# Dividing additions, turns and products by halves of the features in the first block of a two-block transformer kernel

## The chip, the cores and the metric

One core of a Trainium2 chip runs the whole kernel in one launch. The metric is device time in microseconds of that core; smaller is better.

## The reference, cut to what matters

Two transformer blocks of two layers each work on 256 tokens of 1024 features in float32. The change touches only the first block, whose layer is this:

```python
for l in range(DEPTH):                                  # DEPTH = 2
    h = _rms_norm(x, ln1_g[l])
    proj = jnp.einsum('bsd,dn->bsn', h, w_in[l])
    ...                                                 # three attention branches y_a, y_b, y_c
    gates = jax.nn.sigmoid(gate_logits.reshape(b, s, N_BRANCH, d))
    merged = jnp.sum(gates * jnp.einsum('bsne,ned->bsnd', y, w_branch[l]), axis=2)
    x = x + jnp.einsum('bsd,de->bse', merged, w_out[l])
    h2 = _rms_norm(x, ln2_g[l])
    ff = jnp.square(jax.nn.relu(jnp.einsum('bsd,df->bsf', h2, w_ff1[l])))
    x = x + jnp.einsum('bsf,fd->bsd', ff, w_ff2[l])
```

The second block (modulated norms, pooling, convolution, spatial gating, a dense feed-forward and then eight experts) follows and is not edited.

## The kernel before, in words

Tokens lie on partitions in two blocks of 128 (`b`), features along the free dimension in eight groups of 128 (`k`). A product needs its left operand with features on partitions, so TensorE **turns** x or `merged` first: `turn` (L1633 to L1650) makes 16 transposes of 128x128 in four pairs of feature groups, pair 0 and 2 into the PSUM bank T0, pair 1 and 3 into T1. `turned_evac` copies them to `hT`, times the norm's gain: ScalarE takes pairs 0 and 2 (L713 to L717), VectorE pairs 1 and 3 (L1027 to L1031). The norm's row factor is applied later, at the evacuation of the product, so that turning need not wait for it: ScalarE squares and sums x (L703), GpSimd takes the root (L616, L617).

TensorE's order in one layer of the first block is written out by hand, but for two loops of the engine itself (`Fori`): turn x; eight chunks of the projection, two token blocks each (L1680, 372 columns, banks G0 to G3); gates, attention and the products that go with them; the three branch products (L1877), whose result VectorE gates and adds into `merged` (L1309 to L1313); turn `merged`; the output product (L1887), with `k` outermost and the four quarters of x (`j`: half of the features times token block, banks G0 to G3) inside, so that all four quarters end together; VectorE adds the four quarters to x (`add_to_x`, L1041); turn x; the feed-forward, eight chunks of up (L1900, banks S0, S1, T0, T1) and down (L1907, into G0 to G3 across all chunks), opened and closed by four tiny matmuls (L1657, L1661); VectorE adds the four quarters with the squared norm factor (L1043); next layer. VectorE squares the relu's result for each piece of `hid` (L1334).

Weights come through SyncE's queue into a ring of four slots, each loaded when its former user has signalled on `used`. At the start SyncE loads x and then the ring (L510, L516), ScalarE's queue loads `vecs` (gains, tables and the identity matrix, L695), GpSimd's queue the routing table (L603). In layer 1, after the norm factor of the feed-forward, GpSimd's queue also loads what the second block's modulation needs (L646, L626, and twelve chunks of `ada_w`, L631), and VectorE works one or two of these chunks off behind the four squarings of each feed-forward chunk (`ada`, L1074).

## Time and profile before

| | |
|---|---|
| median of 3 runs | 2682.5 us (2679.85 to 2687.35) |
| the profiled execution's own time | 2686.67 us |
| its span | 2684.9 us, mean granted clock 0.969 |
| TensorE busy | 2510.9 us, 94% |
| VectorE, ScalarE, GpSimd busy | 669.6, 340.1, 58.7 us |
| DMA | 619.85 MB, mean 231 GB/s |

The span is the time from the first to the last instruction in the trace, and all starts below count from its beginning. A row gives start and duration in us, the engine, the line of the program, what is written from what, and how many instructions it merges; a float32 product takes two matmul instructions, a transpose one.

### The profile page before, as it was taken

To read this page: it belongs to the slowest core of one execution; us is meant where nothing else is said; L and a number is where in the kernel's file an instruction comes from. 1 tells how busy PE (TensorE), PEld (TensorE's weight loads), DVE (VectorE), ACT (ScalarE), POOL (GpSimd) and SP (SyncE) were. 2 spreads that over 40 slices of the span, in tenths; PEclk is the share of its full clock that TensorE was granted. 3 is DMA by queue.
4 is the path that set the end of the run, shared out by engine and by line. 5 is a ranking of instruction groups with operands and counts; after the bars stand their busy time and mean duration, and the time that the engine had idled before them with its cause. 6 is when DMAs were issued, how large, how long until landed. Compare 5 with 4: busy or idle time off the path is not lost.

```text
span 2684.9 us, 27524 instructions
## 1 busy us (share of the span) xinstructions
PE 2510.9 (94%) x11186; PEld 1579.1 (59%) x11187; DVE 669.6 (25%) x1491; ACT 340.1 (13%) x905; POOL 58.7 (2%) x95
## 2 busy tenths in 40 slices
PE   8999999999999999999999898798998889979997
PEld 5666466656564666666777655447994444434443
DVE  0353200011542243453334541101001101010101
ACT  1242000011530000101000111101000101000101
POOL 0000000000000000000000000000000000000000
PEclk9999999999999999998999898998998999999999
DMA  5323334334233977326664429996655999768971
GB/s 214 127 95 118 135 140 147 142 112 149 94 118 102 342 258 276 130 106 240 262 249 190 187 80 427 421 431 268 277 227 252 429 432 392 293 277 350 395 293 59
DMA packets 71317, 619.85 MB, mean 231 GB/s; under 512 B 4096, under 2 KB 4096, under 8 KB 48816
## 3 DMA queue, kind: packets, MB, share of 16 engines
q1 hardware_dynamic: 57344, 557.33, 52.2%
q0 software_dynamic: 13728, 60.14, 5.9%
q8 instruction: 80, 1.31, 0.2%
q10 hardware_dynamic: 144, 0.90, 0.1%
q14 instruction: 21, 0.17, 0.0%
HBM read 617.31 MB, written 1.05 MB: 230 GB/s over the span
## 4 chain that ended last, share of the span: by engine, by line
PE 82%; DMA 9%; DVE 4%; issue 3%; ACT 2%; POOL 1%; ACTq 0%; DVEq 0%; POOLq 0%; SPq 0%
DMA big<-in_moe_pack 8%; PE G L1907 8%; PE S L2105 7%; PE G L1680 6%; PE S L2103 5%; PE G L1696 5%; PE S L1900 4%; PE T L1900 4%; PE G L2118 4%; PE G L1877 3%; PE S L2040 3%; PE T L2040 3%; PE G L2046 3%; PE G L2116 2%; PE G L1887 2%
## 5 line engine op out<-in xcount | busy, mean ns | idle before, releaser
L2103 PE MATMUL S<-big,hT 128*64 128x256 f32 x2240 | 277.8, 392 | 67.6 <-DMA big<-in_moe_pack 42.2
L2103 PEld LDWEIGHTS S<-big,hT 128*64 128x64 f32 x2240 | 159.9, 140 | 183.5 <-issue 77.8
L1907 PE MATMUL G<-big 128*128 128x512 f32 x512 | 222.3, 592 | 0.0
L1555 DVE TENSOR_TENSOR probs<-S,probs 128x128 f32<-128x128 f32 (+2 forms) x105 | 35.5, 338 | 726.1 <-ACT probs L948 726.1
L2105 PE MATMUL S<-big,hT 128*128 128x512 f32 x448 | 201.3, 592 | 1.2 <-issue 1.2
L1696 PE MATMUL G<-big,hT 128*128 128x384 f32 x512 | 171.0, 488 | 0.0
L1680 PE MATMUL G<-big,hT 128*128 128x372 f32 x512 | 165.8, 488 | 2.5 <-DVE hT L1029 2.5
L1907 PEld LDWEIGHTS G<-big 128*128 128x128 f32 x512 | 97.3, 190 | 115.6 <-issue 114.8
L1074 DVE SCALAR_TENSOR_TENSOR big<-big,small 128x512 f32<-128x512 f32 x192 | 144.2, 751 | 6.5
L2116 PE MATMUL G<-big,pT 128*64 128x512 f32 x560 | 132.3, 593 | 8.3 <-ACT pT L953 8.3
L1680 PEld LDWEIGHTS G<-big,hT 128*128 128x128 f32 x512 | 99.7, 195 | 68.2 <-issue 8.1
L2105 PEld LDWEIGHTS S<-big,hT 128*128 128x128 f32 x448 | 82.8, 190 | 95.6 <-issue 95.6
L1696 PEld LDWEIGHTS G<-big,hT 128*128 128x128 f32 x512 | 95.8, 190 | 65.3 <-issue 4.0
L1900 PE MATMUL S<-hT,big 128*128 128x256 f32 x512 | 117.1, 388 | 0.0
L1900 PE MATMUL T<-hT,big 128*128 128x256 f32 x512 | 113.1, 379 | 0.0
L1900 PEld LDWEIGHTS S<-hT,big 128*128 128x128 f32 x512 | 99.9, 195 | 20.2 <-issue 6.7
L1334 DVE TENSOR_TENSOR big<-big 128x256 f32<-128x256 f32 x64 | 27.2, 426 | 326.0 <-ACT big L861 326.0
L1900 PEld LDWEIGHTS T<-hT,big 128*128 128x128 f32 x512 | 97.3, 190 | 13.2
L2118 PE MATMUL G<-big,pT 128*128 128x512 f32 x224 | 100.9, 593 | 3.3 <-ACT pT L953 3.3
L953 ACT ACTIVATE pT<-T 128x128 f32<-128x128 f32 (+1 forms) x98 | 30.3, 309 | 530.4 <-PE T L2089 530.4
L1877 PE MATMUL G<-big,yT 128*128 128x512 f32 x192 | 82.7, 592 | 0.0
L2040 PE MATMUL S<-hT,big 128*128 128x256 f32 x352 | 81.3, 385 | 0.0
(345 smaller groups left out, 2678.8 us busy)
## 6 DMA issues: line engine op xcount, KB each, us to landing
big<-in_moe_pack SPq DMA_DIRECT2D x112, 3072.0 KB, 15.8
big<-in_w_ff SPq DMA_DIRECT2D x32, 2048.0 KB, 7.9
big<-in_ada_w POOLq DMA_DIRECT2D x24, 2048.0 KB, 14.9
big<-in_ffn_pack SPq DMA_DIRECT2D x11, 3072.0 KB, 10.8
big<-in_gate_pack SPq DMA_DIRECT2D x16, 1536.0 KB, 6.5
big<-in_proj_pack SPq DMA_DIRECT2D x16, 1488.0 KB, 6.2
big<-in_branch_heads SPq DMA_DIRECT2D x6, 2048.0 KB, 7.8
big<-in_w_pack SPq DMA_DIRECT2D x8, 1536.0 KB, 6.2
```

Source lines behind the costliest of these rows:

```text
L1074: dve.scalar_tensor_tensor(out=out, in0=w[:, k, :], scalar=condc[:, k:k + 1], in1=out, op0=ALU.mult, op1=ALU.add).then_inc(ada_step.sem, 1)
L1680: ins = mm(G[2 * (c % 2) + b][:, 0:PROJ_N], hT[:, k, b * P:(b + 1) * P], w[:, k, :], start=(k == 0), stop=(k == KD - 1))
L1696: ins = mm(G[b if n < 4 else 1][:, 0:GATE_N], hT[:, k, b * P:(b + 1) * P], w[:, k, :], start=(k == 0), stop=(k == KD - 1))
L1877: ins = mm(G[j][:, :], yT[:, 4 * n + k, b * P:(b + 1) * P], w[:, k, half * 512:(half + 1) * 512], start=(k == 0), stop=(k == 3))
L1900: ins = mm(H4[f][:, 0:SEQ], w[:, k, f * P:(f + 1) * P], hT[:, k, :], start=(k == 0), stop=(k == KD - 1))
L1907: ins = mm(G[2 * half + b][:, :], hid[:, j, f, b * P:(b + 1) * P], w[:, f, half * 512:(half + 1) * 512], start=False, stop=False, skip_gro ...
L2040: ins = mm(H4[2 * f + piece][:, 0:SEQ], w[:, k, f * SEQ + piece * P:f * SEQ + (piece + 1) * P], hT[:, k, :], start=(k == 0), stop=(k == KD ...
L2046: ins = mm(G[2 * half + b][:, :], ffhid[:, i, f, b * P:(b + 1) * P], dn[:, f, half * 512:(half + 1) * 512], start=False, stop=False, skip_ ...
L2103: ins = mm(S[s % 2][f * FEW:(f + 1) * FEW, 0:SEQ], hTe[:, k, 0:FEW], wt[:, k, f * SEQ:(f + 1) * SEQ], start=(k == 0), stop=(k == KD - 1))
L2105: ins = mm(S[s % 2][:, :], hTe[:, k, 0:P], wt[:, k, :], start=(k == 0), stop=(k == KD - 1))
L2116: ins = mm(G[2][half * FEW:(half + 1) * FEW, :], ehid[:, s % 2, f * FEW:(f + 1) * FEW], wt[:, f, half * 512:(half + 1) * 512], start=first ...
L2118: ins = mm(G[2 + half][:, :], ehid[:, s % 2, f * P:(f + 1) * P], wt[:, f, half * 512:(half + 1) * 512], start=first, stop=last)
```

## The change

1. **Start.** The host also gives x turned (`xT`, features on partitions). SyncE loads `xT` first, then the first chunk of projection weights, then x. `vecs` comes in two parts, the columns with the gains first. ScalarE and VectorE multiply `xT` by the gain straight into `hT`; TensorE turns nothing for layer 0. The routing table is loaded after the first norm's root.
2. **Merging.** `merged_ok` is signalled per half of the features. TensorE turns the first half (pairs 0 and 1) before the last quarter of the last branch product, and the second half after two quarters of the output product.
3. **Output product.** It goes by quarters, first the lower four feature groups of all, then the upper four, and each quarter signals on its own. VectorE adds it to x at once. TensorE turns the first half of x before the last quarter, and the second half after two of the feed-forward's first four pieces, into G0 and G1.
4. **Feed-forward.** TensorE's loop is written out. The first chunk's up products go in two halves of `k`. The last chunk's last two feature groups of the down product go by quarters; in layer 0 the first half of x is turned before the last quarter, and the second half inside the first chunk of layer 1's projection. The tiny opening and closing matmuls go.
5. **Projection.** TensorE's loop is written out too, and its first chunk divided in halves of `k`. ScalarE squares x between its copies of the turned pairs.

```diff
-            sp.dma_start(x[:], t["x"][0].rearrange("(b p) d -> p b d", p=P)).then_inc(x_in.sem, 16)
+            sp.dma_start(xT, t["xT"].rearrange("p (k s) -> p k s", k=KD)).then_inc(xT_in.sem, 16)
...
                 for c in range(8):
                     load(l, c, slot(c)[:, 0:KD * PROJ_N], t["proj_pack"][l, c])
+                    if l == 0 and c == 0:
+                        sp.dma_start(x[:], t["x"][0].rearrange("(b p) d -> p b d", p=P)).then_inc(x_in.sem, 16)
...
-            pool.dma_start(route[:], t["route"]).then_inc(route_in.sem, 16)
...
                 norm_root(l * 2)
+                if l == 0:
+                    pool.dma_start(route[:], t["route"]).then_inc(route_in.sem, 16)
...
-            act.dma_start(vecs[:], t["vecs"]).then_inc(consts_in.sem, 16)
-            act.wait_ge(x_in.sem, 16)
+            act.dma_start(vecs[:, 0:V_BC], t["vecs"][:, 0:V_BC]).then_inc(cols_in.sem, 16)
+            act.dma_start(vecs[:, V_BC:], t["vecs"][:, V_BC:]).then_inc(consts_in.sem, 16)
...
+                if l:
+                    turned_pair(l * 2, 0, xn_turned, T[0], hT_act, gainc[l][0])
+                    square_rows(l * 2, 0)
+                    turned_pair(l * 2, 2, xn_turned, T[0], hT_act, gainc[l][0])
+                    square_rows(l * 2, 1)
...
+            dve.wait_ge(cols_in.sem, 16)
+            dve.wait_ge(xT_in.sem, 16)
+            for i in (1, 3):
+                for k in (2 * i, 2 * i + 1):
+                    ins = dve.tensor_scalar(hT[:, k, :], xT[:, k, :], gainc[0][0][:, k:k + 1], None, ALU.mult)
+                ins.then_inc(hT_dve.sem, 1)
+            dve.wait_ge(consts_in.sem, 16)
+            dve.wait_ge(x_in.sem, 16)
...
-                                if (n, j) == (2, 3):
+                                if n == 2 and b == NB - 1:
                                     ins.then_inc(merged_ok.sem, 1)
                                 else:
                                     step.did(ins)
+                            if (n, j) == (2, 2):
+                                turned_pair(l, 1, mg_turned, T[1], mg_dve, None)
                     if n:
                         step.settle()
-                turned_evac(l, mg_turned, mg_dve, None)
-                dve.wait_ge(used[23 % NSLOT].sem, used_at(l, 23))
-                add_to_x(l * 2 + 1)
-
-                turned_evac(l * 2 + 1, xn_turned, hT_dve, gainc[l][1])
+                turned_pair(l, 3, mg_turned, T[1], mg_dve, None)
+                dve.wait_ge(x_new.sem, added(l * 2))
+                for j in range(4):
+                    if j < 3:
+                        dve.wait_ge(br_mm.sem, br_mm.at(l, 9 + j + 1))
+                    else:
+                        dve.wait_ge(used[23 % NSLOT].sem, used_at(l, 23))
+                    add_quarter(j)
+                    if j == 1:
+                        turned_pair(l * 2 + 1, 1, xn_turned, T[1], hT_dve, gainc[l][1])
+                turned_pair(l * 2 + 1, 3, xn_turned, G[1], hT_dve, gainc[l][1])
...
-                dve.wait_ge(ff2_mm.sem, ff2_mm.at(l, 1))
-                add_to_x(l * 2 + 2, small[:, 306:308])
+                dve.wait_ge(x_new.sem, added(l * 2 + 1))
+                for i, j in enumerate(QUARTERS[l]):
+                    if i < 3:
+                        dve.wait_ge(ff2_mm.sem, ff2_mm.at(l, i + 1))
+                    else:
+                        dve.wait_ge(used[39 % NSLOT].sem, used_at(l, 39))
+                    add_quarter(j, small[:, 306:308])
+                    if (l, i) == (0, 1):
+                        turned_pair(l * 2 + 2, 1, xn_turned, T[1], hT_dve, gainc[l + 1][0])
+                if l == 0:
+                    turned_pair(l * 2 + 2, 3, xn_turned, T[1], hT_dve, gainc[l + 1][0])
...
+            def turn_pair(i, src, bank, turned):
+
+                for kk in range(2):
+                    for b in range(NB):
+                        k = 2 * i + kk
+                        ins = pe.transpose(bank[:, kk * SEQ + b * P:kk * SEQ + (b + 1) * P], src[:, b, k * P:(k + 1) * P], ident[:])
+                ins.then_inc(turned.sem, 1)
...
-                turn(l * 2, x, x_new, added(l * 2), xn_turned, hT_act, hT_dve, whole=False)
...
+                pe.wait_ge(hT_act.sem, hT_act.at(l * 2, 1))
+                pe.wait_ge(hT_dve.sem, hT_dve.at(l * 2, 1))
+                weights(l, 0)
+                pe.wait_ge(proj_act.sem, l * 8 + 1)
+                proj_part(0, 0, 0, KH)
+                if l:
+                    pe.wait_ge(x_new.sem, added(l * 2))
+                    turn_pair(2, x, T[0], xn_turned)
+                    turn_pair(3, x, T[1], xn_turned)
+                pe.wait_ge(proj_dve.sem, l * 8 + 1)
+                proj_part(0, 1, 0, KH)
+                pe.wait_ge(hT_act.sem, hT_act.at(l * 2, 2))
+                pe.wait_ge(hT_dve.sem, hT_dve.at(l * 2, 2))
+                proj_part(0, 0, KH, KD).then_inc(proj_mm.sem, 1)
+                proj_part(0, 1, KH, KD).then_inc(used[0].sem, 1)
+                for c in range(1, 8):
+                    weights(l, c)
+                    pe.wait_ge(proj_act.sem, l * 8 + c + 1)
+                    proj_part(c, 0, 0, KD).then_inc(proj_mm.sem, 1)
+                    pe.wait_ge(proj_dve.sem, l * 8 + c + 1)
+                    proj_part(c, 1, 0, KD).then_inc(used[c % NSLOT].sem, 1)
...
-                turn(l, merged, merged_ok, merged_ok.at(l, 1), mg_turned, mg_act, mg_dve)
...
-                turn(l * 2 + 1, x, x_new, added(l * 2 + 1), xn_turned, hT_act, hT_dve)
-                open_banks()
-                with pe.Fori(0, 4) as it:
...
+                            if (n, j) == (2, 2):
+                                pe.wait_ge(merged_ok.sem, merged_ok.at(l, 1))
+                                turn_pair(0, merged, T[0], mg_turned)
+                                turn_pair(1, merged, T[1], mg_turned)
...
+                pe.wait_ge(mg_act.sem, mg_act.at(l, 1))
+                pe.wait_ge(mg_dve.sem, mg_dve.at(l, 1))
+                weights(l, 21)
+                weights(l, 22)
+                for j in range(4):
+                    pe.wait_ge(br_ev.sem, br_ev.at(l, 8 + j + 1))
+                    if j < 3:
+                        out_part(j, 0, KH)
+                    else:
+                        out_part(j, 0, 3).then_inc(used[21 % NSLOT].sem, 1)
+                        out_part(j, 3, KH)
+                    if j == 1:
+                        pe.wait_ge(merged_ok.sem, merged_ok.at(l, 2))
+                        turn_pair(2, merged, T[0], mg_turned)
+                        turn_pair(3, merged, T[1], mg_turned)
+                pe.wait_ge(mg_act.sem, mg_act.at(l, 2))
+                pe.wait_ge(mg_dve.sem, mg_dve.at(l, 2))
+                weights(l, 23)
+                v = l * 2 + 1
+                for j in range(3):
+                    out_part(j, KH, KD).then_inc(br_mm.sem, 1)
+                pe.wait_ge(x_new.sem, 4 * v + 2)
+                turn_pair(0, x, T[0], xn_turned)
+                turn_pair(1, x, T[1], xn_turned)
+                out_part(3, KH, 6).then_inc(used[22 % NSLOT].sem, 1)
+                out_part(3, 6, KD).then_inc(used[23 % NSLOT].sem, 1)
...
+                for c in range(8):
+                    weights(l, 24 + 2 * c)
+                    if c == 0:
+                        pe.wait_ge(hT_act.sem, hT_act.at(v, 1))
+                        pe.wait_ge(hT_dve.sem, hT_dve.at(v, 1))
...
+                            pe.wait_ge(ff_relu.sem, ff_relu.at(l, f + 1))
+                            up_part(c, f, 0, KH)
+                            if f == 1:
+                                pe.wait_ge(x_new.sem, added(v))
+                                turn_pair(2, x, G[0], xn_turned)
+                                turn_pair(3, x, G[1], xn_turned)
+                        pe.wait_ge(hT_act.sem, hT_act.at(v, 2))
+                        pe.wait_ge(hT_dve.sem, hT_dve.at(v, 2))
+                    for f in range(4):
+                        pe.wait_ge(ff_relu.sem, ff_relu.at(l, 4 * c + f + 1))
+                        up_part(c, f, KH if c == 0 else 0, KD).then_inc((ff_mm if f < 3 else used[2 * c % NSLOT]).sem, 1)
+                    weights(l, 25 + 2 * c)
+                    for f in range(4 if c < 7 else 2):
+                        pe.wait_ge(ff_ev.sem, ff_ev.at(l, 4 * c + f + 1))
+                        for j in range(4):
+                            ins = down_part(c, f, j)
+                    if c < 7:
+                        ins.then_inc(used[(2 * c + 1) % NSLOT].sem, 1)
+                pe.wait_ge(ff_ev.sem, ff_ev.at(l, 32))
+                for i, j in enumerate(QUARTERS[l]):
+                    if (l, i) == (0, 3):
+                        pe.wait_ge(x_new.sem, 4 * (v + 1) + 2)
+                        turn_pair(0, x, T[0], xn_turned)
+                        turn_pair(1, x, T[1], xn_turned)
+                    for f in (2, 3):
+                        ins = down_part(7, f, j)
+                    ins.then_inc((ff2_mm if i < 3 else used[39 % NSLOT]).sem, 1)
```

The order of the instructions shows it at three places; T0, T1, S0, S1 and G0 to G3 are PSUM banks, "waits" names the signals. First TensorE from the last quarter of the last branch product to the output product, before:

```order
L1877 MATMUL G3<-big,yT 128x512 [waits br_ev]
L1877 MATMUL G3<-big,yT 128x512 x3
L1647 MATMUL T0<-vecs,big 128x128 [waits merged_ok]
L1647 MATMUL T0<-vecs,big 128x128 x3
L1647 MATMUL T1<-vecs,big 128x128 x4
L1647 MATMUL T0<-vecs,big 128x128 [waits mg_act]
L1647 MATMUL T0<-vecs,big 128x128 x3
L1647 MATMUL T1<-vecs,big 128x128 [waits mg_dve]
L1647 MATMUL T1<-vecs,big 128x128 x3
L1887 MATMUL G0<-big,hT 128x512 [waits loaded1,mg_dve,mg_act]
L1887 MATMUL G1<-big,hT 128x512
L1887 MATMUL G2<-big,hT 128x512
```

and now:

```order
L1953 MATMUL G2<-big,yT 128x512 [waits br_ev]
L1953 MATMUL G2<-big,yT 128x512 x3
L1721 MATMUL T0<-vecs,big 128x128 [waits merged_ok]
L1721 MATMUL T0<-vecs,big 128x128 x3
L1721 MATMUL T1<-vecs,big 128x128 x4
L1953 MATMUL G3<-big,yT 128x512 [waits br_ev]
L1953 MATMUL G3<-big,yT 128x512 x3
L1965 MATMUL G0<-big,hT 128x512 [waits loaded2,loaded1,br_ev,mg_dve,mg_act]
L1965 MATMUL G0<-big,hT 128x512 x3
L1965 MATMUL G1<-big,hT 128x512 [waits br_ev]
L1965 MATMUL G1<-big,hT 128x512 x3
L1721 MATMUL T0<-vecs,big 128x128 [waits merged_ok]
```

The eight transposes of `merged`'s first half now stand before the last quarter of the branch product, those of the second after two half-quarters of the output product, which is itself reordered. Then TensorE from the output product to the feed-forward, before:

```order
L1887 MATMUL G2<-big,hT 128x512
L1887 MATMUL G3<-big,hT 128x512
L1647 MATMUL T0<-vecs,x 128x128 [waits x_new]
L1647 MATMUL T0<-vecs,x 128x128 x3
L1647 MATMUL T1<-vecs,x 128x128 x4
L1647 MATMUL T0<-vecs,x 128x128 [waits hT_act]
L1647 MATMUL T0<-vecs,x 128x128 x3
L1647 MATMUL T1<-vecs,x 128x128 [waits hT_dve]
L1647 MATMUL T1<-vecs,x 128x128 x3
L1657 MATMUL G0<-zcol,vecs 128x2 [waits hT_dve,hT_act]
L1657 MATMUL G1<-zcol,vecs 128x2
L1657 MATMUL G2<-zcol,vecs 128x2
```

and now:

```order
L1965 MATMUL G2<-big,hT 128x512 x4
L1721 MATMUL T0<-vecs,x 128x128 [waits x_new]
L1721 MATMUL T0<-vecs,x 128x128 x3
L1721 MATMUL T1<-vecs,x 128x128 x4
L1965 MATMUL G3<-big,hT 128x512 x4
L1999 MATMUL S0<-hT,big 128x256 [waits hT_dve,ff_relu,hT_act,loaded0]
L1999 MATMUL S0<-hT,big 128x256 x3
L1999 MATMUL S1<-hT,big 128x256 [waits ff_relu]
L1999 MATMUL S1<-hT,big 128x256 x3
L1721 MATMUL G0<-vecs,x 128x128 [waits x_new]
L1721 MATMUL G0<-vecs,x 128x128 x3
L1721 MATMUL G1<-vecs,x 128x128 x4
```

The turns of x stand apart, each between matmuls that do not wait for it, and the zcol matmuls are gone. Third, VectorE from the additions to x to the feed-forward; `used3` is the last quarter's signal. Before:

```order
L1041 TENSOR_TENSOR x<-G0,x 128x512 [waits x_new,used3]
L1041 TENSOR_TENSOR x<-G2,x 128x512
L1041 TENSOR_TENSOR x<-G1,x 128x512
L1041 TENSOR_TENSOR x<-G3,x 128x512
L1029 TENSOR_SCALAR hT<-T1,vecs 128x256 [waits xn_turned]
L1029 TENSOR_SCALAR hT<-T1,vecs 128x256
L1029 TENSOR_SCALAR hT<-T1,vecs 128x256 [waits xn_turned]
L1029 TENSOR_SCALAR hT<-T1,vecs 128x256
```

and now:

```order
L1068 TENSOR_TENSOR x<-G0,x 128x512 [waits br_mm,x_new]
L1068 TENSOR_TENSOR x<-G1,x 128x512 [waits br_mm]
L1053 TENSOR_SCALAR hT<-T1,vecs 128x256 [waits xn_turned]
L1053 TENSOR_SCALAR hT<-T1,vecs 128x256
L1068 TENSOR_TENSOR x<-G2,x 128x512 [waits br_mm]
L1068 TENSOR_TENSOR x<-G3,x 128x512 [waits used3]
L1053 TENSOR_SCALAR hT<-G1,vecs 128x256 [waits xn_turned]
L1053 TENSOR_SCALAR hT<-G1,vecs 128x256
```

The additions to x stand one by one with their own waits, and the copies of the turned pairs between them.

## Rows read from the trace of the kernel before

**Rows 1.** Chain of waits, whole run: start us, us, engine and line, how many instructions.
```profile
16.26 82.76 PE G L1680 x256
...
256.63 41.22 PE G L1877 x96
303.36 30.02 PE G L1887 x64
341.04 8.70 PE S L1900 x32
349.74 6.91 PE T L1900 x32
356.64 13.73 PE G L1907 x32
...
571.93 83.10 PE G L1680 x256
...
814.34 41.22 PE G L1877 x96
860.61 27.72 PE G L1887 x64
897.68 9.18 PE S L1900 x32
```

**Rows 2.** Chain of waits, from the end of layer 0's feed-forward.
```profile
563.20 0.80 PE G L1661 x8
...
564.03 2.74 DVE x L1043 x4
```

**Rows 3.** Timeline, ScalarE, a projection evacuation: start us, us, engine, line, idle before.
```profile
44.13 0.57 ACT L732 ACTIVATE big<-G,small 128x372 f32 x1 [9.41 <-PE G L1680]
```

**Rows 4.** Chain of waits, first 30 us.
```profile
0.76 7.75 DMA x<-in_x
...
8.68 1.28 ACT L722
...
10.18 2.08 ACT yT L703 x4
```

**Rows 5.** DMA issues of the first 30 us, then one stretch (last columns: PEclk, DMA share, GB/s).
```profile
big<-in_proj_pack SPq DMA_DIRECT2D x5, 1488.0 KB, 13.6
...
vecs<-in_vecs ACTq DMA_DIRECT2D x1, 879.0 KB, 5.8
route<-in_route POOLq DMA_DIRECT2D x1, 232.0 KB, 6.9
...
12.00:16.00 4.00, 1.97 (x8) 1.57 (x8) 0.95 (x3) 1.82 (x6) 0.91 (x2) 1.00 1.01 432
```

**Rows 6.** Timeline, TensorE in attention: transposes, then scores; then that stage's stretch.
```profile
132.08 1.04 PE L1785 MATMUL T<-vecs,probs 128*128 128x128 f32 x8
133.05 1.14 PE L1765 MATMUL S<-big 64*128 64x256 f32 x8
...
124.00:148.00 24.00, 23.00 (x122) 14.11 (x124) 12.29 (x32) 13.86 (x47) 0.00 (x0) 1.00 0.26 97
```

**Rows 7.** Timeline, GpSimd's and VectorE's part in the modulation's chunks; landing of two chunks.
```profile
894.39 1.79 POOL L631 DMA_DIRECT2D big<-in_ada_w  x2
...
DMA to landing us min/median/max: 18.1/20.4/22.6
...
914.56 12.63 DVE L1074 SCALAR_TENSOR_TENSOR big<-big,small 128x512 f32<-128x512 f32 x16
931.40 0.43 DVE L1334 TENSOR_TENSOR big<-big 128x256 f32<-128x256 f32 x1 [4.21 <-ACT big L861]
```

**Rows 8.** Waits of TensorE: us in total, times, longest us.
```profile
PE S L2103 <- issue: 23.5, 4, 10.8
```

**Rows 9.** Stretches after the output product's start, layers 0 and 1.
```profile
303.36:333.38 30.02, 30.01 (x64) 12.97 (x64) 0.00 (x0) 0.00 (x0) 0.00 (x0) 0.92 0.43 158
860.61:888.33 27.72, 27.70 (x64) 12.05 (x64) 0.00 (x0) 0.00 (x0) 0.00 (x0) 1.00 0.55 198
```

More of the change, by code:

```diff
@@ L80 @@
 FT = 2
+KH = KD // 2
+QUARTERS = ((0, 1, 2, 3), (0, 2, 1, 3))
 ROW_L1 = 2 * KD + KCQ + KCKV
@@ L426, in added @@
         def added(n, b=NB - 1):
-            return 4 * n + 2 * b + 2
+            return 4 * n + (3 + b if n < U_MIX else 2 * b + 2)
         def used_at(l, pos):
@@ L1032, in turned_evac @@
-                    ins.then_inc(done.sem, 1)
-            def add_to_x(n, mul=None):
-                dve.wait_ge(x_new.sem, added(n - 1))
-                for b in range(NB):
-                    for half in range(2):
-                        xs = x[:, b, half * 512:(half + 1) * 512]
-                        if mul is None:
-                            dve.tensor_tensor(xs, G[2 * half + b][:, :], xs, ALU.add).then_inc(x_new.sem, 1)
-                        else:
-                            dve.scalar_tensor_tensor(out=xs, in0=G[2 * half + b][:, :], scalar=mul[:, b:b + 1], in1=xs, op0=ALU.mult, op1=ALU.add).then_inc(x_new.sem, 1)
+                    turned_pair(v, i, turned, T[1], done, mul, add)
@@ new lines, in up_part, with down_part @@
+                def up_part(c, f, k0, k1):
+                    w = slot(24 + 2 * c).rearrange("p (k n) -> p k n", k=KD)
+                    for k in range(k0, k1):
+                        ins = mm(H4[f][:, 0:SEQ], w[:, k, f * P:(f + 1) * P], hT[:, k, :], start=(k == 0), stop=(k == KD - 1))
+                    return ins
+                def down_part(c, f, j):
+                    half, b = divmod(j, 2)
+                    w = slot(25 + 2 * c).rearrange("p (k n) -> p k n", k=4)
+                    return mm(G[j][:, :], hid[:, c % 2, f, b * P:(b + 1) * P], w[:, f, half * 512:(half + 1) * 512],
+                              start=(c == 0 and f == 0), stop=(c == 7 and f == 3))
```

137 lines of the change are left out of this document (68 added, 69 removed).

## Prediction

> **What bounds the kernel now.** The table of busy time comes first: TensorE works 94% of the span, so only its idle stretches and its slow stretches can be won. The chain of waits over the whole run is read next [rows 1]. In the first block it is TensorE almost throughout, in long unbroken pieces; what the change can touch are the seams between them. There are five where x or `merged` is turned, and each is the distance from the end of one piece to the start of the next. Merging, layer 0: 256.63 + 41.22 = 297.85 to 303.36, 5.51 us. Merging, layer 1: 855.56 to 860.61, 5.05. Output product to feed-forward, layer 0: 333.38 to 341.04, 7.66. The same in layer 1: 888.33 to 897.68, 9.35. Feed-forward to layer 1's projection: 563.20 [rows 2] to 571.93, 8.73. Together 36.3 us. In the last of them VectorE's four additions, which all start when the last quarter is ready, take 2.74 us alone [rows 2]; the rest is turning, copying and turning again.
>
> Each seam has a second price, seen behind it [rows 1, 9]. After the merging of layer 0 the 64 matmul instructions of the output product take 30.02 us at a granted clock of 0.92; the same in layer 1 takes 27.72 at 1.00. A piece of 32 such instructions takes 13.73 in steady state, so 64 take 27.46: the lower level of the clock (1.2 instead of 2.4 GHz), granted after TensorE stood idle, cost 2.56 and 0.26 us. The first up piece behind the next seam takes 8.70 and 9.18 instead of 6.91: 1.79 and 2.27. The projection of layer 1 takes 83.10; one evacuation of 0.57 and an idle wait of 9.41 make 9.98 us per chunk [rows 3], 79.9 for eight, so 3.2 is lost. Together 10.1 us.
>
> **The start.** x lands at 8.51 and the first product begins at 16.26 [rows 1, 4]; between them lie ScalarE's table load (1.28 us), two squarings that hold up its copies (2.08), and turning in two rounds. With `xT` nothing of this stands before the product but the table load and the multiplications, four to an engine, of which the first two are enough. What stands there instead is the first chunk of weights, until now covered. By 8.51 the queues had moved x (1024 KB), `vecs` (879) and the routing table (232) [rows 4, 5]. Without the table, 232 KB at 432 GB/s earlier, and with the chunk's 1488 KB behind, its weights are there at 8.51 - 0.55 + 3.53 = 11.5; I take 11.6 for the product, a gain of **4.7 us**. Bounds: if the second part of `vecs` takes no share ahead of it, near 9.9 (gain 6.4); if x, queued behind, takes its full share, 2.4 later (gain 2.3). The queues moved what lay ahead and no more by 8.51, so I take the middle. x then lands near 14, is squared by 16.5, and its root is needed only when the first quarter of the projection is complete, some 9 us after its start: hidden. The second chunk of weights, near 17.5, is needed near 24. The products at the low level, which the first ones also were, stay.
>
> **The five seams.** The transposes themselves stay on TensorE. In attention eight of them, between matmuls, take 0.97 us from first start to the next instruction's [rows 6], so 16 take 1.94 and five seams 9.7. All else in the seams I cost at nothing, and name the cover. Merging: the first half is turned after the third quarter of the last branch product; the copies (under 1 us on either engine) lie under the fourth quarter, an eighth of 27.46, 3.4 us. The second half's additions lie under two half-quarters, 6.9 us, its copies under two more. Output to feed-forward: an addition (a quarter of the 2.74 us) lies under the next half-quarter; the first half's copies under the last one; the second half's addition under two up pieces, 3.5 us. There VectorE waits for the turned pair with the third quarter's addition queued behind, which nobody needs before the second turn. Feed-forward to projection: the cover is one down quarter, 1.7 us, for copies of 0.9, the tightest place; then four projection matmuls, 2.5 us. If any cover is short, tenths are lost. So the seams give 36.3 - 9.7 = **26.6 us**, less about 0.1 for each of ten blocks of transposes: **25.6**. Bounds: 26.6, and 21 if each block stands open by 0.5.
>
> **The clock.** With no idle stretch of more than tenths, I take all **10.1 us** back; between nothing and this.
>
> **The end of layer 1's feed-forward.** The closing matmuls (0.80 us, as in layer 0 [rows 2]) go, and three of four additions are done before the last quarter, 2.1 us of 2.74. The next product also waits for the modulation's own matmuls and copies, which move only by the 0.80. I take **1.5**, between 0.8 and 2.9.
>
> **Moved work that might cost.** Slots 2 and 3 of the ring come free together at the end of the output product, instead of apart; their loads are needed 29 us later (one up and one down chunk), so nothing. GpSimd's routing load waits for the first root; nobody asks for it in this block. Layer 1's chunks for the modulation are issued after the norm's root, which now comes after the second turn inside the feed-forward instead of before it. Before, they were issued at 894.39, 3.3 us ahead of the first up product; now at least two up pieces and a turn behind it, 4.4, and by a square (half of 2.08 [rows 4]) and a root more, so some 7: 10 us later. Two chunks landed after 18.1 to 22.6 us and VectorE worked on them from 914.56 for 12.63 us, then stood idle 4.2 us before the next squaring [rows 7]. The squaring's result is needed only by the next down product, another 10 us on. Cost nothing; the rival below has the price.
>
> Sum: 4.7 + 25.6 + 10.1 + 1.5 = 41.9, so **42 us**. The profiled execution's own time, 2686.67, becomes 2644.7; it lay 4.2 above the median of the runs, 2682.5, from which I get 2640.5 and forecast **2641**. The second block only shifts: each of its loads waits for TensorE's own progress.
>
> **Rivals.**
> 1. *The clock falls all the same.* Ten blocks of transposes of a microsecond each might count as standing idle. For it: the low level followed seams in which TensorE turned much of the time. Against it: in attention, with such blocks among the products, the granted clock is 1.00 [rows 6]. It takes the 10.1 us away: 2651. The Trainium skill's page "TensorE: Matmul & The Clock Gate", section "Part 4: PE-mode transpose", says that a transpose does not count as busy in the way a product does; by that rule the time is this rival's. The stretch of attention does not bear it out for short blocks.
> 2. *VectorE is late with the modulation's chunks.* If a chunk is 15 us later, VectorE ends its two chunks after the next down product wants its squares. For it: 4.2 us of slack before the squaring. Against: another 10 us behind it. Price 1 to 8 us: 2646.
> 3. *Gains swallowed later*: a load in the second block that runs by itself would give the time back there. Nothing in the chain shows one; 2682, no change.
> 4. *Slower: written-out code must be fetched.* TensorE's loops ran 16 chunks a layer from two or four bodies; now each chunk has its own code. Where TensorE entered other code in the expert stage it waited for nothing that the profile shows, 23.5 us in 4 times [rows 8], 5.9 each. One such wait in each of 16 feed-forward chunks is 94 us, so 2735; it decides from the eighth wait on. Against it: attention is written out, and TensorE was busy 23.0 of 24 us there [rows 6]. The Trainium skill's page "Runtime: NRT & Kernel Launch", section "Instruction fetch mechanics", says that fetching runs ahead in sequence and that taken branches break it; by this rule the rival falls away. No run here shows fetching by itself.
>
> **Chances.** Forecast 0.72, clock 0.12, VectorE 0.09, swallowed 0.04, fetch 0.03. A measurement tells 0.3% (8 us) from no change; the first three are all faster, 0.93, then 0.04 the same and 0.03 slower. The range takes in the forecast with its bounds (start 1.7 more, end 1.4, blocks 1, and 3 to 5 us between runs: 2630), the clock rival, and that rival with VectorE's price: **2630 to 2660**.
>
> **What would show it.** First product near 11.6; the ends and starts of the pieces 2 us apart at each seam, all of it transposes; the output product, with its turns taken off, at 27.5 us in both layers; first up pieces at 6.9; granted clock 1.00 behind the seams. Layer 1's second feed-forward chunk tells rival 2 by a wait of TensorE for VectorE; a gap without a releaser in the written-out loops tells rival 4. I would be wrong if the seams closed and the span shrank by less than 30 us, or if they stayed open by more than 3 us each.

## The result and the profile after

| | before | changed |
|---|---|---|
| time, median of 4 runs each | 2684.76 us (2679.85 to 2687.35) | 2649.25 us (2644.59 to 2653.8) |
| ratio | | 0.987, 95% interval 0.9846 to 0.9894 |
| profiled execution, its span | 2686.67, 2684.9 | 2649.68, 2647.9 |
| mean granted clock of the span | 0.969 | 0.975 |

The kernel is faster by 35.5 us in the medians and by 37.0 in the two profiled spans. The forecast was 42 off the span, and 2641 with a range of 2630 to 2660 for the time.

First the chain of waits of the changed kernel over the whole run, its long pieces in the first block (start us, us, engine and line, instructions), beside [rows 1]:

```profile
1.20 10.71 DMA big<-in_proj_pack
...
12.16 83.15 PE G L1733 x256
...
254.58 37.77 PE G L1953 x88
...
551.38 77.52 PE G L1733 x248
...
866.83 30.67 DMA big<-in_ada_w
...
904.27 16.27 PE G L2006 x32
...
934.35 13.73 PE G L2006 x32
...
1098.21 7.14 PE G L2077 x32
```

The first product now starts at 12.16, 4.1 earlier, and what it waits for is the first chunk of weights (the row of 10.71). Two rows are new in kind: a DMA of `in_ada_w` stands in the chain at 866.83 for 30.67 us, and the down product behind it takes 16.27 where its neighbours take 13.73. That is the place where the change lost time.

How a seam looks now, first between output product and feed-forward in layer 0, then between feed-forward and projection, from the same view in two short windows:

```profile
321.57 0.88 PE T L1721 x8
322.44 3.44 PE G L1965 x8
325.88 3.45 PE S L1999 x16
329.33 0.87 PE G L1721 x8
330.21 3.46 PE T L1999 x16
...
546.29 1.72 PE G L2006 x4
548.01 2.50 PE G L1733 x8
550.51 0.87 PE T L1721 x8
```

Every row starts where the last one ended. The eight transposes (L1721) take 0.87 or 0.88 us, and nothing else is left of the seam. The windows say the same (PE, PEld, DVE, ACT and POOL busy, then PEclk, DMA share and GB/s); the first three lie over seams, the fourth behind the last of them:

```profile
296.00:342.00 46.00, 46.00 (x158) 27.75 (x157) 8.59 (x18) 6.05 (x14) 0.89 (x2) 1.00 0.51 183
528.00:560.00 32.00, 32.00 (x111) 19.19 (x110) 6.80 (x15) 5.20 (x11) 0.89 (x2) 1.00 0.27 98
828.00:870.00 42.00, 42.00 (x144) 24.93 (x143) 7.57 (x15) 5.29 (x12) 3.98 (x6) 1.00 0.63 228
870.00:905.00 35.00, 30.75 (x109) 20.58 (x108) 14.10 (x22) 2.30 (x6) 1.76 (x2) 0.96 1.03 400
```

TensorE is busy in 46.00 of 46.00, 32.00 of 32.00 and 42.00 of 42.00 us. In the fourth it is busy for 30.75 of 35, while the DMA engines are full (share 1.03, 400 GB/s).

Where the 37.0 us came from, as distances between the starts of pieces in the two chains:

| term | forecast | measured |
|---|---|---|
| first product (16.26 to 12.16) | 4.7 | 4.1 |
| five seams and the clock behind them | 35.7 | 37.5 |
| end of layer 1's feed-forward (15.23 to 12.38) | 1.5 | 2.85 |
| modulation chunks late | 0 | -6.8 |
| all else (layer 0's projection, attention, second block) | 0 | -0.7 |
| sum | 42 | 37.0 |

The second row is made of these: branch product to first up product 84.41 to 71.30 in layer 0 and 83.34 to 71.30 in layer 1; layer 0's feed-forward to the next projection 230.89 to 222.13; layer 1's projection 83.10 to 80.89, its turn included; together 36.1. To these come 1.4 that layer 1's feed-forward would have given without its wait: it took 222.64 before and 228.05 now, and eight periods of 27.55 (the distance between the starts of down products in steady state) with a turn of 0.87 are 221.27. 228.05 - 221.27 is the loss of 6.8.

The loss itself, first in the waits of TensorE between 780 and 1130 us (line waited at, engine and line waited for: us in total, times, longest):

```profile
PE G L2006 <- DVE big L1376: 4.3, 1, 4.3
```

and then in VectorE's timeline, which answers to [rows 7] (start us, us, line, operation, idle before and its releaser):

```profile
889.08 6.26 DVE L1101 SCALAR_TENSOR_TENSOR big<-big,small 128x512 f32<-128x512 f32 x8 [15.73 <-DMA big<-in_ada_w]
897.52 6.27 DVE L1101 SCALAR_TENSOR_TENSOR big<-big,small 128x512 f32<-128x512 f32 x8 [2.18 <-DMA big<-in_ada_w]
903.70 1.43 DVE L1376 TENSOR_TENSOR big<-big 128x256 f32<-128x256 f32 x4
```

VectorE stands 15.73 us waiting for a chunk. Its program puts chunks 0 and 1 ahead of the squarings of the second feed-forward block, so these squarings run as four at once at 903.70, and the down product that wanted the first of them at 900.02 waits 4.3 us. Then it takes 16.27 instead of 13.73: 2.5 us more at the low level. 4.3 + 2.5 is the 6.8.

Why the chunks came so late shows in GpSimd's timeline:

```profile
863.93 0.69 POOL L623 TENSOR_TENSOR small<-small,mhalf 128x2 f32<-128x2 f32 x1
...
865.38 0.56 POOL L632 DMA_DIRECT2D big<-in_ada_bias  x1
865.93 1.79 POOL L637 DMA_DIRECT2D big<-in_ada_w  x2
```

and in the landing of these two chunks:

```profile
DMA to landing us min/median/max: 23.1/26.9/30.7
```

The issue moved from 3.3 us ahead of the first up product to 8.2 behind it (857.78), 11.4 later; the landing of the second chunk grew from 22.6 to 30.7, 8.1 more. In the kernel before, VectorE was still at work on the first chunk for 3 us after the second had landed, and that hid 3 of it. 11.4 + 8.1 - 3.0 = 16.5, and the end of the two chunks indeed lies 46.0 us behind the first up product where it was 29.5. Why the landing grew is told by the queues between issue and landing of the second chunk (queue: packets, MB, share of the 16 engines' time), q0 being GpSimd's, q1 SyncE's. Before, 895.27 to 917.9 us:

```profile
q0 software_dynamic: 1471, 8.38, 93.8%
q1 hardware_dynamic: 279, 0.60, 7.1%
```

and in the changed kernel, 866.83 to 897.5 us:

```profile
q0 software_dynamic: 1472, 8.39, 68.4%
q1 hardware_dynamic: 1496, 3.90, 33.7%
```

GpSimd's queue moves the same in both, the band, the bias and two chunks. SyncE's moves 3.30 MB more, and the engines together 398 GB/s before and 402 now: 3.30 MB are 8.2 us at that rate, the whole growth. 2.10 MB of the 3.90 are the load of weights issued at 872.69, when the first feed-forward chunk's up products are done; it landed after 23.1 us, within the stretch. Most of the rest is left of the two loads issued together at 856.25 and 857.98.

The end of the last feed-forward, in the chain:

```profile
1085.85 0.76 DVE x L1070
```

One addition stands there; before it were the closing matmuls and four additions in a row.

### The profile page after: what moved, and what is told of

Same layout as the page of the kernel before. It is cut to its first block, busy times and chain, and to the rows that moved or that the text cites. A ratio compares the mean times of both kernels' runs of the same rounds, so it can differ in the third digit from the quotient of the medians.

```text
span 2647.9 us, 27348 instructions
## 1 busy us (share of the span) xinstructions
PE 2484.4 (94%) x11138; PEld 1560.8 (59%) x11139; DVE 669.9 (25%) x1491; ACT 340.6 (13%) x906; POOL 58.5 (2%) x95
## 4 chain that ended last, share of the span: by engine, by line
PE 82%; DMA 10%; DVE 3%; issue 2%; ACT 1%; POOL 1%; ACTq 0%; SPq 0%; DVEq 0%; POOLq 0%
DMA big<-in_moe_pack 9%; PE G L2006 8%; PE S L2236 7%; PE G L1733 6%; PE S L2234 5%; PE G L1771 5%; PE S L1999 4%; PE T L1999 4%; PE G L2249 4%; PE G L1953 3%; PE S L2171 3%; PE T L2171 3%; PE G L2177 3%; PE G L2247 2%; PE S L2300 2%
## 5 line engine op out<-in xcount | busy, mean ns | idle before, releaser
L1606 DVE TENSOR_TENSOR probs<-S,probs 128x128 f32<-128x128 f32 (+2 forms) x105 | 35.5, 338 | 729.7 <-ACT probs L975 729.7
L1999 PE MATMUL S<-hT,big 128*128 128x256 f32 x512 | 113.4, 379 | 0.0
L2171 PE MATMUL S<-hT,big 128*128 128x256 f32 x352 | 79.6, 379 | 0.0
```

What stands on the lines that cost most here:

```text
L1999: ins = mm(H4[f][:, 0:SEQ], w[:, k, f * P:(f + 1) * P], hT[:, k, :], start=(k == 0), stop=(k == KD - 1))
L2171: ins = mm(H4[2 * f + piece][:, 0:SEQ], w[:, k, f * SEQ + piece * P:f * SEQ + (piece + 1) * P], hT[:, k, :], start=(k == 0), stop=(k == KD ...
```

## The experiments

**1. Modulation chunks early.** The changed kernel, with the bias and the first two chunks issued in layer 1 as soon as merging is complete, the band later:

```diff
+                if l == DEPTH - 1:
+                    pool.wait_ge(merged_ok.sem, merged_ok.at(l, 2))
+                    load_modulation(0, 0, 2)
...
-            load_modulation(0)
+            load_modulation(0, 2)
```

> The changed kernel, but GpSimd issues the bias and the first two chunks of the modulation's weights as soon as merged is complete in layer 1, before the norm's root; the band table comes behind them. Theory (late chunks): in the changed kernel VectorE waited 15.7 and 2.2 us for chunks, TensorE then 4.3 us for VectorE, and the next down product took 16.27 instead of 13.73 us at the low clock. Without this 6.8 us go: about 2642 against 2649, no wait of TensorE on the squaring, down products at 13.73. Rival (DMA contention): the weights of the output product and the feed-forward, loaded at the same time, come late instead and TensorE waits for them: 2649 or more.

Measured: 2644.76 us (2639.61 to 2645.66), ratio to before 0.9848 (0.9834 to 0.9862). Span 2643.7, that is 4.2 under the changed kernel's. The 6.8 us are all there in layer 1's feed-forward: it takes 221.26 us instead of 228.05, and TensorE waits for no squaring. The edge in question, in VectorE's timeline:

```profile
871.06 12.62 DVE L1105 SCALAR_TENSOR_TENSOR big<-big,small 128x512 f32<-128x512 f32 x16
```

Both chunks are worked on without idle time before them, where the changed kernel had 15.73 and 2.18 us, and are done at 883.68.

Up to the end of that feed-forward this run is ahead of the changed kernel by 9.0 us (1076.84 against 1085.83), of which 2.0 come from the first projection and attention, whose low level differs from one execution to the next (below). Behind it, the next product took 8.77 us instead of 7.14, at the low level, and the second block some 3 us more. So the loss is located and removed, while the total moved by less than the place did.

**2. Chunks late in the kernel before.** The same mechanism from the other side: the band, bias and chunks are held back.

```diff
+            pool.wait_ge(ff_relu.sem, ff_relu.at(DEPTH - 1, 4 + 1))
             pool.dma_start(rot[:, 2048:4096], t["band"]
```

> The kernel before, with GpSimd's loads of the modulation held back until the first relu of layer 1's feed-forward, some 10 us later; nothing else changed. Theory (late chunks): the same loss as in the changed kernel appears without any of its reordering, TensorE waits 3 to 6 us for the squaring and then runs slow: plus 5 to 8 us, 2689 to 2693. Rival (the written-out loop or the quarters caused the wait): no difference from before, 2684.

Measured: 2682.21 us, ratio 0.9998 (0.9988 to 1.0007). No effect; the expectation missed. VectorE's timeline:

```profile
921.91 6.26 DVE L1075 SCALAR_TENSOR_TENSOR big<-big,small 128x512 f32<-128x512 f32 x8 [11.84 <-DMA big<-in_ada_w]
930.05 6.26 DVE L1075 SCALAR_TENSOR_TENSOR big<-big,small 128x512 f32<-128x512 f32 x8 [1.88 <-DMA big<-in_ada_w]
936.24 1.42 DVE L1335 TENSOR_TENSOR big<-big 128x256 f32<-128x256 f32 x4
```

VectorE waits for the chunks as it should, but the squarings begin at 936.24 and the down product that wants them starts at 936.80, less than 0.1 us behind the up product (its end is at 936.74). The slack was used up exactly. The issue lay 8.2 us behind the first up product (900.92 against 892.69), as in the changed kernel, and the second chunk landed after 28.2 us instead of 22.6: SyncE's queue moved 2.92 MB beside it, though its loads are spaced here as before. A later issue thus brings most of the longer landing with it, and the two together use up the slack and no more. The changed kernel's wait needs the rest: its second chunk landed after 30.7 us, and it wants the squares 42.2 us behind its first up product instead of 44.0, because that block no longer runs at the low level. 2.5 and 1.8 are the 4.2 between the two waits, to a tenth.

**3. Two groups later still.** To see whether the wait begins past that edge:

```diff
-            pool.wait_ge(ff_relu.sem, ff_relu.at(DEPTH - 1, 4 + 1))
+            pool.wait_ge(ff_relu.sem, ff_relu.at(DEPTH - 1, 4 + 3))
```

> This is the kernel before with the band, the bias and the modulation chunks of layer 1's feed-forward held back until the third rectified group of the first block, two groups (6.9 us) later than in the run with them held to the first. There the two squarings of VectorE ended in the very microsecond in which TensorE wanted them. Theory (VectorE's order puts two chunks ahead of the squarings, so a chunk that lands later than that run's is paid by TensorE one for one): TensorE waits 6 to 7 us for VectorE's squaring before the down product of the second block, and that product runs at the low level or partly at it for 0 to 2.5 us more; 2689 to 2692 us. Rival (the wait in the changed kernel came from the two queues' collision in the DMA engines, not from order and lateness): no wait of TensorE above 1 us, 2682 to 2685.

Measured: 2695.8 us (2685.65 to 2700.69), ratio 1.0043 (1.0029 to 1.0056). The waits of TensorE, then the chain:

```profile
PE G L1908 <- DVE big L1335: 8.0, 1, 8.0
```

```profile
907.88 29.22 DMA big<-in_ada_w
...
943.88 16.05 PE G L1908 x32
```

Against experiment 2 the chunks are issued 6.8 us later, counted from the first up product, and land after 29.2 us instead of 28.2. That gives 7.8 of the 7.9 more of waiting (8.0 against under 0.1), and again a down product at the low level, 16.05. The chain has the same DMA row as the changed kernel's. The span is 9.8 above the last run's, about what these two make (7.9 and 2.1). The median is 4 us above what was expected; the runs lie over 15 us, and that part is not explained. The rival (collision alone) falls: in the kernel before, whose loads of weights are spaced as ever, order and lateness are enough. No run takes away only the bunching of the two loads that SyncE now issues together. Without it the landing is 28.2 and 29.2 us here and in experiment 2, so it can account for the last 1.5 to 2.5 of the 30.7.

**4. Loops written out.** The kernel before, with TensorE's two hardware loops unrolled and nothing else:

```diff
-                with pe.Fori(0, 2) as it:
+                for it in range(2):
...
-                with pe.Fori(0, 4) as it:
+                for it in range(4):
```

> The kernel before, with TensorE's two loops (projection and feed-forward) written out and nothing moved. Theory: code that runs straight on costs nothing here: 2684, within 3 us. Rival (fetch): gaps of 5.9 us with no releaser in the written-out stretches, slower by tens of us.

Measured: 2686.3 us, ratio 1.0008 (0.9998 to 1.0017). Its waits of TensorE include

```profile
PE S L2103 <- issue: 24.0, 5, 10.7
```

as in [rows 8] (23.5 us): no new gap without a releaser in the feed-forward. Up to 1130 us, where the written-out loops stand, its matmuls have no wait of 0.3 us or more without a releaser. Writing out costs nothing that can be measured, at most 4.6 us by the interval.

**5. The start alone.** The kernel before with `xT`, `vecs` in two parts, and the routing table later:

```diff
-            sp.dma_start(x[:], t["x"][0].rearrange("(b p) d -> p b d", p=P)).then_inc(x_in.sem, 16)
+            sp.dma_start(xT, t["xT"].rearrange("p (k s) -> p k s", k=KD)).then_inc(xT_in.sem, 16)
...
+            act.wait_ge(cols_in.sem, 16)
+            act.wait_ge(xT_in.sem, 16)
+            for i in (0, 2):
+                for k in (2 * i, 2 * i + 1):
+                    ins = act.activation(hT[:, k, :], xT[:, k, :], ACT.Copy, scale=gainc[0][0][:, k:k + 1])
```

> The kernel before with the start of the changed kernel alone: x loaded turned, gains first, routing table later. Theory: the first product starts at 12.2 instead of 16.3, all else follows 4 us earlier: 2680.5 or so. Rival (the start was hidden by something later, or the later x holds up the first evacuation): no difference, 2684.

Measured: 2677.64 us against 2682.89, ratio 0.998 (0.9971 to 0.9989). The chain starts

```profile
1.20 10.62 DMA big<-in_proj_pack
...
11.94 1.60 PE G L1701 x2
```

so 4.3 us earlier than 16.26, and the median agrees (5.2 lower).

**6. Seams filled.** The kernel before keeps its seams, but TensorE multiplies an unused tile in them, into a bank that nobody reads:

```diff
+            def fill(n):
+                for _ in range(n):
+                    mm(S[1][:, 0:384], ident[:], vecs[:, 0:384], start=True, stop=True)
```

> The kernel before, with idle time in the five seams filled by matmuls whose result nobody reads (identity times the gain columns, into bank S1): two ahead of the first turn of merged and four ahead of that of x, one or two in the later waits of a turn. The output is unchanged. Theory (the low clock behind a seam comes from idle time): the clock stays up, the pieces behind the seams take 27.5, 6.9 and 80 us; of the 10.1 us some 8 to 10 come back, less 1 or 2 for fillers that overrun: 2675 to 2679. Rival (the clock falls for another reason, such as the transposes): the pieces stay slow, and the time is 2684 or up to 4 us more.

Measured: 2675.98 us, ratio 0.9969 (0.9958 to 0.9981), 7.2 us in medians, without closing a single seam. The pieces behind the seams:

```profile
304.78 27.72 PE G L1895 x64
...
340.14 7.01 PE S L1908 x32
...
568.52 80.23 PE G L1688 x256
...
889.65 7.01 PE S L1908 x32
```

against 30.02, 8.70, 83.10 and 9.18 in [rows 1]. With the idle time filled and the transposes left in place the pieces run at full speed, so here it was idle time that lowered the clock. But the other runs on the kernel before, whose seams stand open (experiments 2 to 5), show that two of these four rows were a draw: a low level that one profiled execution has and another of the same code has not. The output product of layer 0 took 29.71 in experiment 2 and 27.72 in the other three, and layer 1's projection took 80.25 to 80.28 in all four. Only the first up piece is slow every time (8.70 to 9.41 us behind layer 0's seam, 9.18 to 9.60 behind layer 1's). So what is lost reliably is 1.8 to 2.7 us behind the output seam in each layer. Of the forecast's 10.1, 5.2 (30.02 - 27.72 and 83.10 - 80.25) are lost in some executions and not in others. The low level also lengthens the seams from within: in layer 1's output seam of the kernel before, eight transposes took 1.98 us and eight closing matmuls 1.84, and with fillers 1.11 and 1.02. The five seams, 36.3 us long before, are 33.3 here, so some 3.0 of what the forecast counts as seams was clock. The low level behind a seam that is filled or closed was seen in none.

**7. x turned whole.** The changed kernel with the seam between output product and feed-forward put back:

```diff
-                turn_pair(0, x, T[0], xn_turned)
-                turn_pair(1, x, T[1], xn_turned)
...
+                turn(v, x, x_new, added(v), xn_turned, hT_act, hT_dve)
...
-                                turn_pair(2, x, G[0], xn_turned)
-                                turn_pair(3, x, G[1], xn_turned)
```

> The changed kernel, but x is turned whole between output product and feed-forward, after all four additions, with the quarters of the output product kept. Theory: the seam opens again by the last addition (0.7), two rounds of copies (about 1 and 1.1) and the clock falls in some of the two: plus 3 to 5 us a layer, 2655 to 2659. Rival (only ending the product by quarters mattered, the halves of the turn did nothing): within 2 us of the changed kernel's 2649.

Measured: 2650.79 us, ratio 0.9883 (0.9868 to 0.9898), 1.5 above the changed kernel instead of 6 to 10. By the total this is the rival's number, but the chain tells otherwise. It shows the seam (the output product ends at 322.30):

```profile
301.68 20.62 PE G L1964 x48
...
326.81 3.69 PE S L1996 x16
```

From branch product to the next layer's projection it is 296.43 us instead of 293.43: 3.0 lost in layer 0. In layer 1 the same distance to the end of the feed-forward is 295.79 instead of 299.35: 3.6 gained. TensorE has no wait for a squaring there, and the second down product takes 13.95. The seam gives the modulation's chunks the time that they lack, and so hides its own price.

**8. x turned whole and chunks early.** Experiments 7 and 1 together, to see the seam without that cover:

> This is the changed kernel with both single edits together: x turned whole between output product and feed-forward, and the first two modulation chunks fetched early in layer 1. Theory (the seam itself costs 3.0 us in each layer, 6.0 in all, and the run with x turned whole alone came out only 1.5 us above the changed kernel because the same edit removed the 6.8 us that TensorE had waited and run slowly for the chunks): with the wait gone on both sides, branch product to the end of the last down product in layer 1 takes 292.5 + 3.0 = 295.5 us here, the same 3.0 us longer branch product to layer 1's projection in layer 0 (296.4), and the run is about 6 us above the 2644.8 of the early chunks alone, 2649 to 2652. Rival (the divided turn of x gains nothing, the seam is worth under 1 us): 2644 to 2647, with stretches of 293.4 and 292.5 us.

Measured: 2650.07 us, ratio 0.9869 (0.9853 to 0.9885), 5.3 above the 2644.76 of the early chunks alone. In the chain, from branch product (254.19) to projection (548.90 + 1.72 = 550.62) 296.43 us; from branch product in layer 1 (789.09) to the end of the feed-forward (1084.66) 295.57, against 292.56 in experiment 1: 3.0 us for each of these seams, as expected. The rows of experiment 7 give the same price: the seam from 322.30 to 326.81 is 4.51 us, turning included, then TensorE takes 3.69 instead of 3.45 for 16 matmuls, and saves two blocks of transposes, 1.75, of the divided version. 4.51 + 0.24 - 1.75 = 3.0. This prices the divided turn of x alone. What ending the output product by quarters gave, and the seams of merging and of the next projection, is read from the chain and was not taken back by itself.

**9. Transposes fourfold.** The changed kernel with each block of eight transposes issued four times:

```diff
-                for kk in range(2):
+                for kk in range(2 * 4):
+                    kk = kk % 2
```

> The changed kernel with each block of eight transposes repeated four times in place (it writes the same values again; output unchanged). Nine such blocks of 0.87 us become 3.5 us each. Theory (transposes keep the clock up like other matmuls): plus 9 times 2.6, 23 us, 2672, granted clock 1.00 behind the blocks. Rival (transposes count as idle): matmuls behind the blocks run at the low level, 2 to 3 us more for each, 2690 to 2699.

Measured: 2665.18 us, ratio 0.9939 (0.9924 to 0.9955); span 2663.4, 15.5 more than the changed kernel's, at a mean granted clock of 0.978. One seam, from the chain:

```profile
303.19 3.49 PE T L1722 x32
306.69 17.17 PE G L1966 x40
323.86 3.50 PE T L1722 x32
...
330.79 3.45 PE S L2000 x16
```

A block takes 3.5 us, 2.62 more, and every product behind one runs at full speed: 17.17 for 40, 3.45 for 16. The window over this stretch has clock 1.00:

```profile
296.00:342.00 46.00, 46.00 (x198) 29.49 (x197) 6.89 (x14) 4.52 (x10) 0.89 (x2) 1.00 0.51 182
```

From branch product to projection layer 0 takes 306.54 instead of 293.43, five blocks of 2.62. Ten blocks, where the expectation counted nine, make 26.2. The total grew by only 15.5, not by the 23 expected, because layer 1's chunks are again less late (TensorE waits 1.3 us instead of 4.3, and the down product takes 13.97), 5.2 us in all, and because start, first projection, attention and second block happen to be 5.5 shorter. The rival, that transposes let the clock fall, is not borne out.

**10. The best version.** Experiment 1, with the second part of `vecs` issued by ScalarE after its copies of `xT`, so that it takes no share ahead of the first weights:

```diff
-            act.dma_start(vecs[:, V_BC:], t["vecs"][:, V_BC:]).then_inc(consts_in.sem, 16)
...
                 ins.then_inc(hT_act.sem, 1)
+            act.dma_start(vecs[:, V_BC:], t["vecs"][:, V_BC:]).then_inc(consts_in.sem, 16)
```

> The early chunks of the other run, and the second part of vecs (687 KB) issued by ScalarE after its copies instead of at once. Theory: the first weights land some 1.6 us earlier (687 KB at 432 GB/s), first product near 10.5, the gains at 9 to 10 just cover it: 2640 to 2641. Rival: hT, ready near 9.8, or the tables, needed by VectorE, hold up something: no better than 2642.

Measured: 2639.29 us (2637.68 to 2643.66), ratio 0.984 (0.9827 to 0.9853), span 2637.5, 10.4 under the changed kernel's.

```profile
1.20 8.93 DMA big<-in_proj_pack
...
10.37 2.82 PE G L1737 x4
```

1.8 us come from the start (10.37 against 12.16), 6.8 from layer 1's feed-forward; the rest is 2.7 from the first projection and attention, where the low level is a draw, less 0.9 elsewhere. All five runs of it lie below every run of the changed kernel.

## Why the prediction held, and where it was off

**The start** was read rightly, by its middle: 4.1 of 4.7. That the second part of `vecs` takes part of the share ahead of the weights, kept in the forecast as the bound of 6.4, is what the last experiment turns into 1.8 us.

**The seams** closed as forecast. No cover ran short, the tightest one of 1.7 us for copies of 0.9 included. The transposes were the over-costed part: taken at 0.97 from attention, and at 0.1 more for each block, they cost 0.87. Two per seam in five seams, 1.07 - 0.87 each, make 2.0 us, and that is why seams and clock gave 37.5 instead of 35.7. (The lower bound for open blocks, 26.6 less ten times 0.5, is 21.6 and not 21.)

**The clock** came back in full, as the step said; the filled seams show that idle time was its cause. Some 3.0 us of the 26.6 booked as seams were clock as well (experiment 6). But of the 10.1 us I read from one profiled execution, about half was not there in the other executions of the same seams. The two spans, from which 37.0 comes, contain it, and the medians (35.5) only in part. A low level that is a draw shows in attention as well. There scores of eight instructions behind a wait take 1.94 and 1.99 us at the low level, 1.14 and 1.13 else: in layer 1 before, in layer 0 after. With the eight behind them (1.71 and 1.69 instead of 0.86) it costs 1.7 us in either kernel and cancels. That row, of the changed kernel's chain in layer 0:

```profile
120.23 1.94 PE S L1840 x8
```

The one place of [rows 6], a little later in the same layer before, ran at the full level.

Rival 1 falls: blocks of up to 3.5 us of transposes between products did not bring the granted clock down (1.00 in experiment 9). The Trainium skill's page "TensorE: Matmul & The Clock Gate", section "Part 4: PE-mode transpose", says that a transpose does not count as busy in the way a product does; this kernel does not bear that out for blocks of this length, and longer ones were not tried.

**The end** gave 2.85 where I took 1.5, the upper of the two bounds. The one addition left takes 0.76 us ([rows 2] had 2.74 for four).

**The chunks** are the step that failed: "Cost nothing; the rival below has the price". Rival 2, at 0.09, came true, and its price of 1 to 8 us holds the 6.8. The slack was read rightly, 4.2 before the squaring and some 10 behind it. What was mis-sized is how late the chunks would be: 10 us were forecast and 16.5 came, against 14. The issue was 11.4 later, near enough. But the landing was taken to be as it was, and it grew by 8.1, because SyncE's queue moved 3.90 MB beside it instead of 0.60. Of this some 5.6 us come with the later issue itself (experiment 2) and up to 2.5 with the two loads that now go out together. The sentence about these, "needed 29 us later, so nothing", priced them for their own consumer only, and not for who shares the DMA engines with them. A price was also missing from the wait: the low level in the down product behind it, 2.5 us, which the argument on the seams should have supplied. Experiments 1 to 3 show the mechanism from both sides: taken away, 6.8 gained in place; made in the kernel before, nothing up to the edge and then one for one.

**Swallowed later** (rival 3) falls, since the second block took 1549.69 us after 1549.35. **Fetch** (rival 4) falls by experiment 4. The Trainium skill's page "Runtime: NRT & Kernel Launch", section "Instruction fetch mechanics", says that fetching runs ahead in sequence, and experiment 4 agrees: no wait of 0.3 us or more without a releaser in the written-out loops, and a ratio of 1.0008.

**The total** is in part luck: seams and end gave 3.2 us more than forecast, which covers nearly half of the 6.8. The profiled execution lies 5.0 above the 2644.7 forecast for it. The rest of the 8.8 by which the median, 2649.25, lies above 2640.5 is the step from execution to median: 4.2 was taken off, and it was 0.4.

## What to carry to other kernels

When a change closes idle time, ask which transfers that idle time was covering: everything that is issued on a fixed event now has fewer microseconds until its consumer. Cost a later issue with both its parts, the shift and the landing, and count in the landing every byte that the other queues will move beside it at its new time (here 8.39 and 3.90 MB at 402 GB/s make the 30.7 us). And read the clock's price from several executions, since a piece at the low level in one profile may be a draw. The idle time ahead of a piece did not tell by itself whether it pays: in the kernel before TensorE was idle for 4.45 us in layer 0's output seam and for 4.55 ahead of layer 1's projection, and the up piece behind the first lost 1.8 us or more in every execution profiled with open seams, while the projection lost 3.1 in one of five and some 0.3 in the others (80.02 in the changed kernel taken as full speed). Why stays open.

## What the runs showed that was not expected

The slack was sharp to a fraction of a microsecond: held to the first group, TensorE waited less than 0.1 us; held to the third, 8.0. A wait of 4.3 us and one of 8.0 both brought the low level for the product behind them (16.27 and 16.05 for 32 instructions), while the waits of under 0.1 and of 1.3 us in experiments 2 and 9 did not (13.97 both, against 13.73). And putting a seam back cost 1.5 us in the total where it stood open for 3.0 in each layer, because it repaired a wait elsewhere: an edit that is undone alone tells only its net, and the second edit beside it was needed to see the price.
